# The last level of a blocked triangular inversion, on blocks of 64 rows and 64 columns

## The reference, cut to what matters

```
kk = jnp.einsum('bhnid,bhnjd->bhnij', kc, kc)
a_mat = jnp.where(causal_mask(c, strict=True), beta[..., :, None] * kk * gamma, 0.0)
t_mat = a_mat + jnp.eye(c, dtype=f32)
u = lax.linalg.triangular_solve(t_mat, vc * beta[..., None], ...)
w = lax.linalg.triangular_solve(t_mat, kc * (beta * jnp.exp(cum))[..., None], ...)
```

## Time and profile before

| | us |
|---|---|
| median of 3 runs | 2796.62 (2795.85 to 2799.03) |
| the profiled execution | 2794.27 |
| its span, first to last instruction | 2792.4 |
| TensorE busy (matmuls) / weight loads | 2656.4 / 2339.5 |
| VectorE / ScalarE / GpSimd busy | 1895.7 / 993.9 / 499.7 |

### The profile page before, as it was taken

How to read it: one execution, slowest core, us unless ns; L and a number is a source line. 1 busy time by engine, 2 the same in 40 slices (tenths; PEclk the granted TensorE clock), 3 DMA queues, 4 the chain that set the end, 5 groups by cost and what they waited for, 6 DMA issues and landing times.

```text
span 2792.4 us, 44953 instructions
## 1 busy us (share of the span) xinstructions
PE 2656.4 (95%) x16632; PEld 2339.5 (84%) x16632; DVE 1895.7 (68%) x3625; ACT 993.9 (36%) x2228; POOL 499.7 (18%) x433
## 2 busy tenths in 40 slices
PE   7999999999999999999998999987999999999998
PEld 3789889889888988988997998887978888888887
DVE  4577767867867776776776776765566666666656
ACT  4543653464374364345336326332430000000002
POOL 0000410220130031000000000000044344333341
PEclk9999999999999999999999999989999999999999
DMA  6221121122122112212212212223122111111111
GB/s 203 61 57 31 43 59 46 31 58 57 20 58 67 28 40 58 48 32 67 54 30 52 58 28 64 63 64 111 33 61 61 46 46 53 53 46 46 46 46 61
DMA packets 222619, 152.44 MB, mean 55 GB/s; under 512 B 27857, under 2 KB 207033, under 8 KB 222401
## 3 DMA queue, kind: packets, MB, share of 16 engines
q1 hardware_dynamic: 209728, 141.70, 17.7%
q0 software_dynamic: 12672, 7.87, 2.9%
HBM read 133.28 MB, written 16.26 MB: 54 GB/s over the span
## 4 chain that ended last, share of the span: by engine, by line
PE 68%; DVE 21%; ACT 8%; issue 2%; DMA 1%; SPq 0%; DVEq 0%; ACTq 0%
PE bank L179 26%; PE bank L171 16%; PE bank L2053 8%; DVE feat_region L1616 3%; DVE sig L1047 2%; PE bank L968 2%; PE bank L1193 2%; PE bank L1185 2%; DVE wB_lo L1100 1%; DVE wA_lo L1100 1%; PE bank L1127 1%; PE bank L1140 1%; PE bank L443 1%; DVE feat_region L1341 1%; PE bank L1513 1%
## 5 line engine op out<-in xcount | busy, mean ns | idle before, releaser
L171 PE MATMUL bank<-wB_hi,h_hi 128*128 128x256 f32 x1024 | 301.2, 294 | 9.3 <-ACT conv_in L1004 6.9
L171 PE MATMUL bank<-wA_hi,h_hi 128*128 128x256 f32 x1024 | 297.9, 291 | 10.7 <-ACT conv_in L1004 5.8
L171 PE MATMUL bank<-wB_lo,h_hi 128*128 128x256 f32 x1024 | 301.6, 295 | 0.0
L171 PE MATMUL bank<-wB_hi,h_lo 128*128 128x256 f32 x1024 | 299.8, 293 | 0.0
L171 PE MATMUL bank<-wA_lo,h_hi 128*128 128x256 f32 x1024 | 297.1, 290 | 0.0
L171 PE MATMUL bank<-wA_hi,h_lo 128*128 128x256 f32 x1024 | 296.8, 290 | 0.0
L179 PE MATMUL bank<-h_hi,wA_hi 128*128 128x512 f32 x672 | 267.4, 398 | 2.7 <-DVE feat_region L981 2.2
L179 PE MATMUL bank<-h_hi,wB_lo 128*128 128x512 f32 x672 | 267.7, 398 | 0.0
L179 PE MATMUL bank<-h_hi,wA_lo 128*128 128x512 f32 x672 | 267.4, 398 | 0.0
L179 PE MATMUL bank<-h_hi,wB_hi 128*128 128x512 f32 x672 | 267.4, 398 | 0.0
L179 PE MATMUL bank<-h_lo,wA_hi 128*128 128x512 f32 x672 | 266.5, 397 | 0.0
(11 more groups left out here) (391 smaller groups left out, 6217.1 us busy)
## 6 DMA issues: line engine op xcount, KB each, us to landing
w_raw<-in_w_in_dram SPq DMA_DIRECT2D x96, 512.0 KB, 3.9
w_raw<-in_w_ffn_up_dram SPq DMA_DIRECT2D x44, 512.0 KB, 3.8
rows_region<-in_ada_w_dram SPq DMA_DIRECT2D x64, 256.0 KB, 2.7
w_raw<-in_w_ffn_down_dram SPq DMA_DIRECT2D x22, 512.0 KB, 3.5
rows_region<-in_x_dram SPq DMA_DIRECT2D x8, 512.0 KB, 7.7
w_raw<-in_w_in_dram SPq DMA_DIRECT2D x16, 256.0 KB, 2.9
y_scratch<-ybuf SPq DMA_DIRECT2D x32, 128.0 KB, 1.8
y_scratch<-ybuf POOLq DMA_DIRECT2D x32, 128.0 KB, 3.2
```

The lines of the kernel that those rows point to most:

```text
L171: mm = nc.tensor.matmul(bank[:, n_out:n_out + n1 - n0], (h_hi, h_lo)[hp][:, k, t * P:t * P + P], buf[wp][:, k, n0:n1], start=(s == 0), sto ...
```

## The change

At b = 64 alone, both products are taken on the quarter that counts, 64 rows and 64 columns of the weights in place of 128 and 128. Phase 0 takes rows 0 to 63 of the triangle and of `xm`, and writes partitions 64 to 127 of the bank. Phase 1 takes rows 64 to 127 of `pm` and `xmt`, and writes partitions 0 to 63. VectorE's masked multiply at this level becomes a plain copy of 64 partitions, its subtraction is made on 64 partitions. The number of instructions, their order, the semaphores and the DMAs stay the same, and the five lower levels too.

```diff
--- before.py
+++ after.py
@@ -43,6 +43,7 @@
 SMALL = GLA_RANK + 2 * ML_H + 2 * GDN_H
 LEVELS = [2, 4, 8, 16, 32, 64]
 BLOCK = 32
+H64 = 64
 HALF = S // 2
 MAX_SEMS = 157
 
@@ -1182,7 +1183,12 @@
                 pe.wait_ge(sem("gdn_x"), 6 * D_ + v + 1)
                 pe.wait_ge(sem("gdn_xt"), 7 * D_ + v + 1)
                 for c in range(2):
-                    last = mm(M[3][:, c * 64:c * 64 + 64], at[:, c, 0:P], one(xm[:, c], b, 0), start=True, stop=True)
+                    if b == H64:
+                        last = mm(M[3][H64:P, c * 64:c * 64 + 64], at[0:H64, c, H64:P], xm[0:H64, c, 0:H64], start=True,
+                                  stop=True)
+                    else:
+                        last = mm(M[3][:, c * 64:c * 64 + 64], at[:, c, 0:P], one(xm[:, c], b, 0), start=True,
+                                  stop=True)
                 last.then_inc(sem("gdn_p"), 1)
             else:
                 pe.wait_ge(sem("gdn_pm"), 6 * D_ + v + 1)
@@ -1190,8 +1196,12 @@
                     if 2 * b == P // 2:
                         mm(M[3][:, 128 + c * 64:192 + c * 64], xmt[:, c], one(pm[:, v, c], b, 0), start=True,
                            stop=True)
-                    last = mm(M[3][:, 256 + c * 64:320 + c * 64], pm[:, v, c], one(xmt[:, c], b, 1), start=True,
-                              stop=True)
+                    if b == H64:
+                        last = mm(M[3][0:H64, 256 + c * 64:320 + c * 64], pm[H64:P, v, c, 0:H64],
+                                  xmt[H64:P, c, H64:P], start=True, stop=True)
+                    else:
+                        last = mm(M[3][:, 256 + c * 64:320 + c * 64], pm[:, v, c], one(xmt[:, c], b, 1), start=True,
+                                  stop=True)
                 last.then_inc(sem("gdn_q"), 1)
         elif j >= TILE0:
             c, s = divmod(j - TILE0, 3)
@@ -1326,6 +1336,10 @@
 
             if phase == 0:
                 dve.wait_ge(sem("gdn_p"), 6 * D_ + v + 1)
+                if b == H64:
+                    step(dve.tensor_copy(pm[H64:P, v, :, 0:H64], M[3][H64:P, 0:128].rearrange("p (c n) -> p c n", c=2)),
+                         "gdn_pm")
+                    return
                 mask = level_mask[:, v].rearrange("p (n b) -> p n b", b=b).unsqueeze(1).broadcast_to([P, 2, n, b])
                 step(tt(pair(pm[:, v], b, 0), cols(0), mask, ALU.mult), "gdn_pm")
                 if v == 2:
@@ -1336,7 +1350,11 @@
                 dve.wait_ge(sem("gdn_q"), 6 * D_ + v + 1)
                 if 2 * b == P // 2:
                     step(tt(pair(xm[:], b, 0), pair(xm[:], b, 0), cols(128), ALU.subtract), "gdn_x")
-                step(tt(pair(xmt[:], b, 1), pair(xmt[:], b, 1), cols(256), ALU.subtract), "gdn_xt")
+                if b == H64:
+                    step(tt(xmt[0:H64, :, H64:P], xmt[0:H64, :, H64:P],
+                            M[3][0:H64, 256:384].rearrange("p (c n) -> p c n", c=2), ALU.subtract), "gdn_xt")
+                else:
+                    step(tt(pair(xmt[:], b, 1), pair(xmt[:], b, 1), cols(256), ALU.subtract), "gdn_xt")
                 if 2 * b <= BLOCK:
                     step(dve.transpose(xm.rearrange("p c n -> p (c n)"), xmt.rearrange("p c n -> p (c n)")), "gdn_x")
         elif j >= TILE0:
```

## The result

The changed kernel took 2802.97 us (median of 13 runs, 2798.0 to 2807.43), the kernel before 2796.62 (13 runs, 2793.54 to 2799.63): 1.0023 times as long, 95% interval 1.0015 to 1.0031, so 6.4 us more. The forecast was 2803.3.

A forecast was written before the change was run, and what follows sets the result against it. TensorE bounds the kernel (95% of the span, 68% of the chain). Drains and uncovered loads, less shorter loads, add 0.12 us at each of 56 groups: 2796.62 + 6.7 = 2803.3 us, range 2795.0 to 2810.0.

The forecast's parts named there:

- The group's pace is set by its loads: Last level (block 64), four matmul instructions per group: loads of 64 columns cut each from 0.112 to 0.058 us.
- Every change of form drains, and uncovers a load: Around each last-level group: the next load starts 0.07 us before the last matmul's end and is uncovered, on both sides.
- The sum of 0.81 us and 1.03 us: Time around one last-level group between 256- and 512-column projection matmuls, against 0.69 and 0.91 before: 0.12 us more.
- The rival built on the rule of TensorE: Matmul & The Clock Gate: Last-level groups: no drain, only shorter loads, 0.216 us less each, 12.1 us less in all, 2784.5; chance 0.10.
- 56 of 64 groups reach the end: Last-level groups with the chain on TensorE: 56 x 0.12 = 6.7 us added to the end.
- the wait that was named: TensorE's 1.78 us wait for line 1349, after the first four heads' fourth pairs, swallows 0.24 us.
- One count: Last level: 24 of the 32 pairs stand among 256-column projection matmuls and 8 among 512-column ones.
- VectorE's edit is worth nothing: Last level: the 64-partition copy takes about 291 ns for the masked multiply's 292; the subtraction is also taken as unchanged.
- The rival of a dearer change: Last-level groups: drains add up or gaps lower the clock more often, 56 x 0.24 = 13.4 us, 2810; chance 0.12.
- The half-drain rival: Last-level groups: only one side drains, some -0.05 us a group, -3 us, or slack takes it; 2793 to 2802; chance 0.18.
- The chance of 0.61 for a slowdown beyond 0.2%: Whole kernel slower than 2802.2 us: 0.49 from both switches draining as summed, and the dearer case.
- One sign: Profiled span longer by 6 to 8 us, spread evenly over 150 to 1900 us of the trace, none behind it.

The follow-up runs named there:

- the repeat: The changed kernel measured again, on one chip with its first-four-heads and last-four-heads versions, against new runs of the kernel before: 1.0024 times (1.0015 to 1.0032).
- the first four kernels: Four follow-up kernels, each run in turn with the kernel before on the same chip; the text does not list which four.

## Why the prediction was right

**The group's pace is set by its loads:** right. The small loads take 133 to 138 ns for 192.

**Every change of form drains, and uncovers a load:** right, and the step that decided. The form of 64 rows by 64 columns was in no row; three other forms were, and gave the same 0.07 us. The sum of 0.81 us and 1.03 us stands in the trace as 0.805 and 1.03, and the loader is idle for 0.07 us behind each group of the first 31 pairs. The rule of TensorEngine Tiling (Array Packing) of the Trainium skill, under Key Properties, that changing the tiling mode drains TensorE, holds here for rows alone, for columns alone and for both. The rival built on the rule of TensorE: Matmul & The Clock Gate of the Trainium skill, under LDWEIGHTS, that loads take time by their columns, was right in that rule: 80 columns gave 0.12 us a group back, and 64 rows took nothing off the pace of the loads. It fell only because 64 columns change the form.

**56 of 64 groups reach the end:** right within what can be told: the half in the first four heads and the half in the last four add up to the whole, and the wait that was named took up 0.24 us in each of four places. The last-heads half should be the dearer by 0.9 us, which these intervals can't tell. One count is off by little: 23 pairs stand among 256-column matmuls, not 24. In the 32nd, TensorE waits for VectorE's line 1875 right behind each group (1.27 and 1.00 us, unchanged with the small product), and the load behind is hidden in that wait: with phase 1 alone small, the time from one of these waits to the next went from 2.99 to 2.96 us. So 54 groups cost 0.12, about 6.4 us in all instead of 6.7.

**VectorE's edit is worth nothing:** right for the copy, 295 ns for 292, and the same time with the mask kept. The subtraction got 8 ns shorter, which the sum had at nothing; for 32 of them that is 0.3 us of VectorE's time.

**The rival of a dearer change** named drains that add up where rows and columns both change; columns alone cost as much as both, so they don't. Its other ground, gaps that lower the granted clock, showed little: the mean over the 13 runs is 0.9873, for 0.988 over the runs of the kernel before beside the experiments, and 0.9871 for 0.9883 in the repeat, which by the line above is 1 to 2 us, part of the 6.4 and 7.7. The half-drain rival fell with the 0.21 and the 0.07 on either side of the group.

**The range** was 2795 to 2810, the measurement 2802.97 and its repeat 2803.28. That the median lies 0.3 us from the forecast is luck: its interval is 4.2 to 8.7 us above the kernel before. The chance of 0.61 for a slowdown beyond 0.2% was about as the numbers allowed; 0.23% is just past it, and the interval reaches to both sides of 0.2%. One sign did not come as named: the profiled span grew by 10.4 us, not by 6 to 8, and not evenly, since 4.4 of them came in the 65 us from the 32nd pair's last level on, with the lower clock.

## What to carry to other kernels

A small product among full ones is not priced by its size but by whether it changes the form in which the array is used; here that cost 0.33 us a group, against 0.21 that its shorter loads gave back. Look in the trace for any product of few rows or few columns, and at when the load behind it starts. Where a product needs only part of its columns, cut the weights just so far that the form stays: with 80 columns a group of this kernel gains the 0.12 us that it loses with 64.

## What was not expected of the hardware

Where the form stays, the first load of a group costs nothing, with 80 columns as with 128, because it runs under the matmul ahead: 80 columns saved 3 x 0.04 us and not 4 x 0.04.

Where the form changes could be read off the trace of before. In line 1513, whose weights grow from 16 to 128 columns in steps of 16, the next matmul starts 0.15 us before the recorded end of the one ahead at every step but two: from 32 to 48 and from 64 to 80 columns it is 0.07, 32 times each. So 64 columns and 80 lie on two sides of a change here, and 80, 96, 112 and 128 on one. It doesn't hold for every narrow product: behind line 179's float32r matmuls with 40 columns a full one starts 0.16 us before the end of the last, at the one place where nothing else holds it up.

And the mean granted clock moves single runs of this kernel more than the change does: the 34 runs of the kernel before beside the first four kernels spread over 17 us (2789.03 to 2806.04), which is why a change of 0.2% needed ten and more runs.
